# Embedding products from split operands, half of them issued later, and an identity matrix written on the chip

## What is computed

```python
z = rmsnorm(h, ln_in) @ w_in                  # c_q, c_kv, k_r, g_a, u_val, u_gate, g_c
o_a = ...                                     # multi-head latent attention over 8 heads
y_a = rmsnorm(o_a * jax.nn.silu(g_a), ln_out_a)
v = causal_dwconv(u_pad, conv_w, conv_b)      # 31 taps per channel, 512 channels
v = jax.nn.silu(layernorm(v, ln_conv_g, ln_conv_b))
y_c = rmsnorm(v * jax.nn.silu(g_c), ln_out_c)
h = h + jnp.concatenate([y_a, y_c], axis=-1) @ w_out
gate = jax.nn.sigmoid(rmsnorm(h, ln_pg) @ w_pg)
h = h + gate * (p @ w_pe)                     # p: 640 x 256, w_pe: 256 x 1024
```

## Time and profile before

| | |
|---|---|
| median of 3 runs | 765.39 us (765.08 to 766.03) |
| the profiled execution's own time | 765.02 us |
| its span | 762.9 us |
| PE busy | 749.0 us (98%) |
| DVE busy | 562.0 us (74%) |
| ACT busy | 428.2 us (56%) |

### The profile page before, as it was taken

How to read it: one execution, slowest core, us unless ns; L and a number is a source line. 1 busy time by engine, 2 the same in 40 slices (tenths; PEclk the granted TensorE clock), 3 DMA queues, 4 the chain that set the end, 5 groups by cost and what they waited for, 6 DMA issues and landing times.

```text
span 762.9 us, 10602 instructions
## 1 busy us (share of the span) xinstructions
PE 749.0 (98%) x3749; PEld 601.8 (79%) x3749; DVE 562.0 (74%) x1084; ACT 428.2 (56%) x996; POOL 91.6 (12%) x161
## 2 busy tenths in 40 slices
PE   9999999999999999999999999999999999999995
PEld 7899887767777588888888988877678767888874
DVE  3459978979877986546453798988888879655577
ACT  3865655665566733263366575647655758223564
POOL 1500323420001400000000020353000000000000
PEclk9999999999999999999999999999999999999998
DMA  8742222410011343412282223233111014332203
GB/s 271 229 128 83 88 73 86 115 36 15 35 35 28 123 167 130 134 56 83 66 279 77 91 76 85 82 81 83 41 36 43 1 54 154 110 125 74 88 5 138
DMA packets 50681, 70.69 MB, mean 93 GB/s; under 512 B 15582, under 2 KB 28154, under 8 KB 50614
## 3 DMA queue, kind: packets, MB, share of 16 engines
q1 hardware_dynamic: 44746, 59.27, 24.6%
q0 software_dynamic: 5824, 10.73, 5.2%
q10 hardware_dynamic: 60, 0.02, 0.0%
HBM read 60.79 MB, written 9.27 MB: 92 GB/s over the span
## 4 chain that ended last, share of the span: by engine, by line
PE 89%; DVE 6%; ACT 2%; DMA 1%; issue 1%; SPq 0%; POOL 0%; ACTq 0%
PE acc L692 20%; PE acc L701 20%; PE acc L698 19%; PE sharedT L616 5%; PE acc L836 5%; PE sharedS L930 4%; PE sharedO L944 4%; PE sharedO L616 2%; PE sharedS L616 2%; DVE VT L1623 2%; PE sharedT L902 1%; PE sharedS L888 1%; PE sharedO L874 1%; PE sharedS L889 1%; PE sharedO L913 1%
## 5 line engine op out<-in xcount | busy, mean ns | idle before, releaser
L692 PE MATMUL acc<-WHI,XHI 128*128 128x512 f32 (+1 forms) x710 | 304.7, 429 | 0.8 <-ACT WHI L1115 0.5
L701 PE MATMUL acc<-WHI,XLO 128*128 128x512 f32 (+1 forms) x710 | 274.7, 387 | 0.0
L698 PE MATMUL acc<-WLO,XHI 128*128 128x512 f32 (+1 forms) x710 | 274.3, 386 | 0.0
L1623 DVE SCALAR_TENSOR_TENSOR VT<-UX,CWT,VT 128x640 f32<-128x640 f32 x240 | 211.5, 883 | 5.0
L692 PEld LDWEIGHTS acc<-WHI,XHI 128*128 128x128 f32 x710 | 133.7, 188 | 29.8 <-issue 6.2
L1553 DVE SCALAR_TENSOR_TENSOR WLO<-WR,GT,WHI 128x512 fp32r<-128x512 f32 (+1 forms) x142 | 98.7, 737 | 78.8 <-ACT WHI L1115 78.6
L698 PEld LDWEIGHTS acc<-WLO,XHI 128*128 128x128 f32 x710 | 133.9, 189 | 27.3 <-issue 6.2
L701 PEld LDWEIGHTS acc<-WHI,XLO 128*128 128x128 f32 x710 | 133.3, 188 | 26.2
L1115 ACT ACTIVATE WHI<-WR,GT 128x512 fp32r<-128x512 f32 (+1 forms) x142 | 93.4, 708 | 85.5 <-PE acc L701 85.3
L1336 ACT ACTIVATE SB<-SB,NBIAS 128x128 f32<-128x128 f32 (+2 forms) x80 | 44.4, 555 | 37.0 <-DVE NBIAS L1682 35.6
L1115 ACT ACTIVATE PT<-sharedT 128x384 f32<-128x384 f32 (+1 forms) x80 | 35.6, 444 | 37.1 <-PE sharedT L616 36.9
(11 more groups left out here) (213 smaller groups left out, 884.4 us busy)
## 6 DMA issues: line engine op xcount, KB each, us to landing
WR<-in_w_in_dram SPq DMA_DIRECT2D x32, 256.0 KB, 3.1
WR<-in_w_in_dram SPq DMA_DIRECT2D x16, 512.0 KB, 3.7
WR<-in_w_out_dram SPq DMA_DIRECT2D x16, 512.0 KB, 3.7
WR<-in_w_pg_dram SPq DMA_DIRECT2D x16, 512.0 KB, 3.5
H<-in_x_prompt_dram SPq DMA_DIRECT2D x16, 256.0 KB, 5.2
WR<-in_w_in_dram SPq DMA_DIRECT2D x8, 416.0 KB, 5.8
residual_spill<-H SPq DMA_DIRECT2D x5, 512.0 KB, 3.4
H<-residual_spill SPq DMA_DIRECT2D x10, 256.0 KB, 3.4
```

What stands on the lines that cost most here:

```text
L692: mm(out, hi, w_hi, start=(first and k == 0), stop=False)
L698: mm(out, hi, w_lo, start=False, stop=False)
L701: last = mm(out, lo, w_hi, start=False, stop=(final and k == 1))
L1623: stt(out=out, in0=src, scalar=w, in1=out, op0=ALU.mult, op1=ALU.add).then_inc(conv_done, 1)
```

## The change

It has four parts. The embedding blocks become split blocks like the others: `PTR` is split into `XHI` (ACT, two copies in unit 22) and `XLO` (POOL, two subtractions), rows 4 and 5, and the weight pieces get `high` and `low`. Block pe1 is moved behind oa0. Around it DVE's and ACT's lists are rewritten, and `TAP` moves single taps between units. At the start, POOL writes the identity, so that x is SP's first transfer, and `zeros(7)` becomes `zeros(5)`.

```diff
-BLOCKS = ["u0", "zA", "u1", "ga", "gc", "cv", "pe0", "pe1", "oa0", "oa1", "oc0", "oc1", "pg0", "pg1"]
+BLOCKS = ["u0", "zA", "u1", "ga", "gc", "cv", "pe0", "oa0", "pe1", "oa1", "oc0", "oc1", "pg0", "pg1"]
...
-PARTS = [c for c in CHUNKS if c[1][:2] != "pe"]
+PARTS = CHUNKS
...
-TAP["turn"] = _take(1)
-
-for _u, _m in enumerate((2, 1, 0, 4, 1, 1, 4, 2, 1, 2, 0, 2, 1, 1, 4, 2, 1, 2, 0, 2, 1, 1, 4, 1, 0, 1, 1, 3)):
+TAP["turn"] = _take(2)
+
+for _u, _m in enumerate((1, 1, 1, 3, 1, 1, 4, 2, 1, 2, 0, 2, 1, 1, 4, 2, 1, 2, 0, 2, 1, 1, 4, 1, 1, 1, 1, 2)):
...
             if l == 0:
-                sp.dma_start(IDENT[:, :], a["c_ident"]).then_inc(ident_in, 16)
...
                 pe.wait_ge(warm_set, 1)
-                zeros(7)
-                pe.wait_ge(ident_in, 16)
+                zeros(5)
+                pe.wait_ge(ident_set, 2)
...
-            copied_wait(pe, (l, "p2"))
-            embed(0, 0)
+            pe.wait_ge(p_low, 2 * (l + 1))
+            quantum("pe0", 0, 0)
             values(UNITS - 1)
...
             for t in range(1, TILES):
-                embed(1, t)
-                turn_ya(t - 1)
+                quantum("pe0", 0, t)
+                if t > 1:
+                    turn_ya(t - 2)
             for c in range(2):
                 for t in range(TILES):
                     copied_wait(pe, (l, ("y", t, 0)))
                     quantum("oa0", c, t)
-                    if (c, t) == (0, 0):
-                        turn_ya(TILES - 1)
+                    if c == 0 and t < 2:
+                        turn_ya(t + 3)
+            for t in range(TILES):
+                quantum("pe1", 0, t)
...
+            def embeddings_high():
+
+                part_used(act, PART[l, "gc", 2])
+                for k in range(2):
+                    copy(XHI[:, :, 4 + k, :], PTR[:, k, :].rearrange("p (t e) -> p t e", e=P)).then_inc(p_high, 1)
...
+                if u == 22:
+                    embeddings_high()
+                if u in (28, 30):
+
+                    high(first_i + 20 + (u - 28) // 2)
...
+            embedding_out(0, 4)
+            high_half((l, ("y", 2, 0)))
+            high(first_i + 22)
...
+            v_tanh_out(0)
+            v_tanh_out(1)
+            high(first_i + 23)
...
+            for t in range(TILES):
+                embedding_out(1, t)
+                if t == 0:
+                    high(first_i + 24)
                 if t == 1:
-                    v_tanh_out(1)
...
+                    v_tanh_out(4)
             for t in range(TILES):
                 act.wait_ge(yc_ready, TILES * l + t + 1)
                 mean_square(Y[:, t, 512:1024], 20 + t, 512)
-            high(first_i + 22)
-            high(first_i + 23)
+            high(first_i + 25)
...
                 taps(TAP.get(NB + u, [])[early:])
+                if u >= 30:
+
+                    low(first_i + u - 10)
...
             norm_of_y(0)
-            low(first_i + 22)
+            low(first_i + 23)
             for t in range(TILES):
                 onto_residual("oa0", t)
-            low(first_i + 23)
+                if t in (1, 2):
+                    conv_gate(t)
+                    normed(t + 2)
+            low(first_i + 24)
+            conv_gate(3)
+            conv_gate(4)
+            low(first_i + 25)
             norm_of_y(1)
...
+            nc.gpsimd.memset(IDENT[:, :], 0.0).then_inc(ident_set, 1)
+            pool.wait_ge(ident_set, 1)
+            nc.gpsimd.affine_select(IDENT[:, :], IDENT[:, :], [[-1, P]], ALU.not_equal, 1.0, base=0,
+                                    channel_multiplier=1).then_inc(ident_set, 1)
...
+            for k in range(2):
+                pool.wait_ge(p_high, 2 * l + k + 1)
+                nc.gpsimd.tensor_tensor(XLO[:, :, 4 + k, :], PTR[:, k, :].rearrange("p (t e) -> p t e", e=P),
+                                        XHI[:, :, 4 + k, :].bitcast(F32), ALU.subtract).then_inc(p_low, 1)
```

More of the change, by code:

```diff
@@ L311, in build @@
         p_in = sem("p_in")
+        p_high = sem("p_high")
+        p_low = sem("p_low")
         wq_rot = sem("wq_rot")
@@ L529, in piece @@
                 if j >= RAW:
[L530 to L534, removed]
+                    before = CHUNKS[j - RAW]
+                    sp.wait_ge(split_ready, PART[before] + 1)
                 load_piece(sp, j)
             if l == 0:
-                sp.dma_start(IDENT[:, :], a["c_ident"]).then_inc(ident_in, 16)
                 for t, g in FIRST_X:
@@ L826, in filler @@
                     quantum(name, c, t, (k,))
[L828 to L839, removed]
             def turn_conv(t):
@@ L1445, in scalar_layer, with ya_square @@
             act.wait_ge(conv_done, CONVS * (l + 1))
[L1446 to L1451, removed]
+            def ya_square(t):
                 act.wait_ge(ya_ready, TILES * l + t + 1)
                 mean_square(Y[:, t, 0:512], 15 + t, 512)
-                if t == 1:
-                    v_tanh_out(1)
[L1456 to L1463, removed]
+            embedding_out(0, 0)
+            embedding_out(0, 1)
+            ya_square(0)
+            embedding_out(0, 2)
+            high_half((l, ("y", 0, 0)))
+            ya_square(1)
+            embedding_out(0, 3)
+            high_half((l, ("y", 1, 0)))
+            embedding_out(0, 4)
+            high_half((l, ("y", 2, 0)))
+            high(first_i + 22)
+            high_half((l, ("y", 3, 0)))
+            ya_square(2)
+            high_half((l, ("y", 4, 0)))
+            ya_square(3)
+            ya_square(4)
+            v_tanh_out(0)
+            v_tanh_out(1)
+            high(first_i + 23)
+            v_tanh_out(2)
+            v_tanh_out(3)
+            for t in range(TILES):
+                embedding_out(1, t)
+                if t == 0:
+                    high(first_i + 24)
+                if t == 1:
+                    v_tanh_out(4)
             for t in range(TILES):
@@ L1471, in scalar_layer @@
                 if t == 0:
-                    high(first_i + 24)
-            for i in range(25, 28):
+                    high(first_i + 26)
+            for i in range(27, 30):
                 high(first_i + i)
@@ L1512, in scalar_layer @@
                 copied_wait(act, (l + 1, "gain"))
-                high(first_i + 36)
+                high(first_i + 38)
             def scaled(t):
@@ L1824, in vector_layer @@
             low_half((l, ("y", 0, 0)))
-            conv_gate(0)
-            for t in (1, 2, 3):
-                low_half((l, ("y", t, 0)))
-            conv_gate(1)
-            low_half((l, ("y", 4, 0)))
-            low(first_i + 21)
-            for t in (2, 3, 4):
-                conv_gate(t)
+            norm_of_conv()
+            low_half((l, ("y", 1, 0)))
+            low_half((l, ("y", 2, 0)))
+            norm_of_conv_end()
+            low(first_i + 22)
+            low_half((l, ("y", 3, 0)))
+            normed(0)
+            low_half((l, ("y", 4, 0)))
+            normed(1)
+            conv_gate(0)
+            normed(2)
             def norm_of_y(group):
@@ L1857, in vector_layer @@
                 if t == 0:
-                    low(first_i + 24)
+                    low(first_i + 26)
                 if t > 1:
@@ L1862, in vector_layer @@
             onto_residual("oa1", 4)
-            low(first_i + 25)
-            low(first_i + 26)
+            low(first_i + 27)
+            low(first_i + 28)
             for t in range(TILES):
@@ L1867, in vector_layer @@
                 if t == 3:
-                    low(first_i + 27)
+                    low(first_i + 29)
                 if t > 1:
@@ L1872, in vector_layer @@
             low_half((l, ("h", 4, 0)))
-            low(first_i + 28)
+            low(first_i + 30)
             for t in range(TILES):
@@ L1900, in vector_layer @@
             if last:
-                low(first_i + 35)
+                low(first_i + 37)
                 dve.wait_ge(lnf_in, 16)
@@ L1907, in vector_layer @@
             else:
-                low(first_i + 34)
-                low(first_i + 35)
+                low(first_i + 36)
+                low(first_i + 37)
                 gains(l + 1)
```

52 lines of the change are left out of this document (25 added, 27 removed).

## The result

The changed kernel takes 768.16 us (median of 9 runs, 766.51 to 770.58), the kernel before 765.26 us in the same comparison (9 runs, 764.79 to 766.03). The ratio is 1.0042, 95% interval [1.0029, 1.0055]: slower by 0.4%, where 764.8 was forecast. The profiled execution took 767.93 us, its span is 766.1 us, 3.2 more than before.

The account below looks back on a forecast made before the run. PE, busy 98%, was taken as the bound, with DVE's list full behind the attention. The terms, -0.44 + 2 x (-0.7 - 0.64 - 3.5 + 4.8) = -0.5, gave 764.8 us, range 758.5 to 767.5.

Parts of the forecast that it names:

- What PE saves: Embedding tiles: 1.37 us as split quanta instead of 1.72, so 3.5 us a layer, 7.0 in all.
- What DVE does to it: Behind the attention: PE waits for additions to H, y's last tile and low part 25, 4.8 us a layer.
- A: Rival, the forecast itself: DVE's list takes back what PE saves; own range 763.3 to 766.5, chance 0.48.
- B: Rival: PE stays the bound, additions and low part 25 in time, new waits 0; 755.2 us, chance 0.12.
- C: Rival: half of the waits, low part 25 in time, third and fourth additions a microsecond earlier; 760, chance 0.22.
- POOL's two subtractions: Low parts of the embeddings' operand: at least 0.6 us each, over 20 us of cover until 243.99, priced at nothing.
- Rival E: POOL slows DVE: four taps of 0.88 double where POOL subtracts, 1.5 us a layer; 767.8, chance 0.06.
- D: Rival, slower: a moved split misses its hole, making unit 31's exponential late; up to 768.7, chance 0.12.
- The clock: At the start: with two fewer zeros a later clock rise would double the first quanta, held for under 1 us.
- The taps: One tap fewer in units 3 and 27: 0.7 us at unit 4 and 0.64 at unit 31's exponential, each layer.
- The preparation by ACT, low parts 20 and 21: ACT's copies in unit 22 hidden; high parts fit ACT's holes of 1.84 and 1.46, low parts DVE's of 1.75 and 1.33.
- The start: SP's transfers go out 0.44 us earlier without the identity before them; taken as -0.44, bounds 0 and -0.6.

Follow-up runs that it names:

- e3: Changed kernel with oa0's five additions together on VectorE, ahead of gates 0 to 4 and norms 2 to 4, ScalarE's list to suit: 757.54 us.
- e6: The kernel before with the new table of taps alone: 761.06 us, ratio 0.9945.
- e2: Changed kernel with 4 extra matmuls before pe1's third quantum and 7 before its fourth, into an unused PSUM bank: 766.60 us.
- e8: Changed kernel with oa0's additions together and early, and the two subtractions moved from GpSimd to VectorE in units 28 and 29: 755.66 us.
- e5: The kernel before with the change's start alone (identity by GpSimd, x as SP's first transfer, five zeros): 764.60 us, ratio 0.9993.
- e10_gp_twice: Changed kernel with each of GpSimd's two subtractions made twice: 774.78 us, ratio 1.0130.

## Why the prediction was wrong

The forecast was -0.5 us, the measurement +2.9. (From 765.39 its sum gives 764.9 rather than 764.8, which changes nothing.) The step that failed is the price of GpSimd's subtractions, which the sum put at nothing; a second, smaller one is the clock, which had no term. Step by step:

- **What PE saves** (3.5 a layer): right in kind, somewhat large. With no waits for additions the stretch is 46.95 where it was 49.79 (e3), 2.8; the wait of 0.3 for y's last tile is in this, so 3.1 against 3.5.
- **What DVE does to it** (4.8 a layer): right. The additions began at 266.04, 0.9 earlier than forecast, the whole being about 1 us earlier by then; the waits were 0.99 and 1.78 for accumulators, 0.41 for low part 25 and 0.19 for y4 by their brackets, and in all 51.54 - 46.95 + 0.3 = 4.9 us. (The brackets come to less than the whole. They count from the modelled end of the matmul before, 0.16 later than the next could have started, and the first matmul behind a wait costs 0.34 where others cost 0.23.) So A was the mechanism of this part, and B and C are excluded for it.
- **"POOL's two subtractions ... I take nothing"**: this step failed. They cost VectorE 2.2 us a layer and TensorE 1.4 (attention 132.13 and 132.26, against 130.70 and 130.80 in e6, which has the same taps). Bounding their price "by cover alone" asked only whether the result would be in time, which it was by 22 us, and not what the instruction does to its neighbour. The Trainium skill (GPSIMD Engine Reference, Key points) had it: the two engines share SBUF interfaces, with contention for VectorE instructions with two SBUF inputs. The trace agrees, at 1.91 and 2.06 for a tap of 0.9; and the prediction's own sign of being wrong, taps near 219 us that take longer than 0.88, came true. Rival E, at a chance of 0.06 and priced at 1.5 a layer, was this. Its reason for the price was not: it doubled four taps, where two were lengthened. That its 767.8 lies near the 768.16 is in part luck, since the three other errors (the clock +1.6, the saving +0.8, the taps -1.3) add 1.1; and D's 768.7 is luck altogether, for nothing that D names happened.
- **The clock**: the prediction spoke of it at the start only. The sum took the waits of pe1 at their own length. In the profiled execution 3.4 us of work behind them ran at the lower level, 53.11 - 51.54 = 1.6 us; e2, which only fills the waits, is 1.3 to 1.6 us faster in the median. No rival had it.
- **The taps** (0.7 and 0.64 a layer): under-sized. They bring 2.0 a layer (e6), 4.0 in all against 2.7. In the changed kernel, too, the masks run 0.8 us ahead of before at the first attention unit, 1.4 at unit 2 and 2.0 at unit 5: 1.2 gained where the earlier trace rows shows a stall of 0.64. Unit 4 has no idle time any more, as forecast; what came before it in unit 2 I had not looked for.
- **The preparation by ACT, low parts 20 and 21** (D): right; they fit their holes, and attention in e8 is that of e6 with these in it.
- **The start** (-0.44): about right. The timeline of PE, beside the earlier trace rows, shows x's first tile transposed at 3.75, where 4.3 was forecast, and the first quantum at 6.25:

```profile
3.75 1.11 PE L620 MATMUL sharedT<-IDENT,H 128*128 128x128 f32 x4
...
6.25 0.47 PE L696 MATMUL acc<-WHI,XHI 128*128 128x512 f32 x1 [0.30 <-ACT WHI L1106]
```

  By the first mask it is 0.93 in this execution; over runs (e5) it is -0.4, in an interval that holds no change too.

With the two missed costs at their measured size the sum closes: 764.8 + 2 x 1.4 for GpSimd + 1.6 for the clock - 2 x 0.66 for the taps + 2 x 0.4 for the smaller saving = 768.7, against 768.16. That the clock's fall takes 1.3 to 1.6 us of the median is shown by e2; which executions it strikes is open: the waits were alike in both layers and only one fell.

## What to carry to other kernels

An idle engine is not free: before moving work to GpSimd, look at what VectorE executes in that time. If that has two inputs in SBUF and GpSimd reads SBUF too, let the VectorE instruction end 0.68 us behind GpSimd's (for this size) and see who waits for it: here a subtraction cost 1.0 to 1.2 us, a copy 0.2 to 0.3, a memset nothing. When a block is put where it needs accumulators back sooner, rewrite the list of the engine that frees them first: what is waited for comes ahead of what is not, and here that, with ScalarE's list to suit, was worth some 10 us, the clock's fall included. And count a wait on TensorE not only by its length but by what may run at half the clock behind it; change one part at a time where one can, since a table of small numbers was the best of this change and was hidden by the rest.

## What was not expected of the hardware

- Beside a subtraction of 128x640 on GpSimd, VectorE's scalar_tensor_tensor of the same size takes 1.91 to 2.06 us instead of 0.89; beside a copy 1.06 to 1.22; beside a memset 0.89. In all 28 such pairs of the profiles (subtractions in five kernels, copies in one) the tap ends 0.67 to 0.68 us behind GpSimd's instruction, whether that reads one operand or two. It works both ways: a subtraction that met a tap ends 1.39 to 1.42 us behind the tap, and takes 1.99 to 2.14 where one that began alone takes 1.55; a copy ends 0.58 behind it. The rows fit two engines that read SBUF in turns; that they do is an inference from these distances.
- TensorE's granted clock fell to 0.50 behind two waits of 0.99 and 1.78 us that lay 1.7 us of work apart, in some executions and layers and not in others, though TensorE had no idle time of over 0.2 us in the 27 us before them. After a single wait of 3.17 us (e10_gp_twice, first layer) it did not fall, after one of 3.18 (second layer) it did. Filling the waits with 11 matmuls brought the spread of the runs from 4.1 to 1.1 us.
